# Seven block products for eight in eight dense stages of a four-block model, and two edits in its gated delta rule

## The reference

```python
h_lat = layer_norm(DEEPNORM_ALPHA * h_lat + mod_lat[2] * y_lat, ln1_g[i], ln1_b[i])
f_lat = swiglu(modulate(h_lat, mod_lat[3], mod_lat[4]), w_ffn_in[i], w_ffn_out[i])
# gated delta rule, per token
# S_t = exp(g_t) (I - beta_t k_t k_t^T) S_{t-1} + beta_t k_t v_t^T,  o_t = S_t^T q_t
```

## Time and profile before

| | |
|---|---|
| median of three runs | 5027.18 us |
| profiled execution | 5031.29 us |
| its span, first to last instruction | 5028.8 us |
| TensorE matmul busy | 4424.2 us (88%) |
| VectorE busy | 1856.6 us (37%) |
| ScalarE busy | 1095.0 us (22%) |
| GpSimd busy | 1299.0 us (26%) |
| mean granted TensorE clock | 0.927 |
| moved over HBM | 104 GB/s over the span |

### The profile page before, as it was taken

The page is one execution under the profiler, slowest core; times in us unless marked ns, Lnnn a source line. Parts: engine busy times, 40 slices in busy tenths (PEclk is TensorE's granted clock), DMA queues, the critical chain, the costliest instruction groups (busy, mean ns, idle before and its releaser), DMA issues. The chain is left out here.

```text
span 5028.8 us, 50281 instructions
## 1 busy us (share of the span) xinstructions
PE 4424.2 (88%) x18452; PEld 2709.6 (54%) x18452; DVE 1856.6 (37%) x3562; ACT 1095.0 (22%) x2335; POOL 1299.0 (26%) x1510
## 2 busy tenths in 40 slices
PE   7889899999898656888989999988899888677998
PEld 4566555555455545775434444556655465563443
DVE  6523555511455672432047502034400209900001
ACT  3143200000211542443010001016600122140001
POOL 1100499876000388200039300020000000350000
PEclk9999999999898776888999999999999999778999
DMA  5401466643110244332248512100011153773221
GB/s 185 151 1 54 122 193 201 190 139 120 42 50 31 78 151 119 82 86 66 72 131 247 191 69 73 56 32 1 0 50 45 59 182 127 249 218 111 76 74 67
DMA packets 245067, 526.64 MB, mean 105 GB/s; under 512 B 141088, under 2 KB 147744, under 8 KB 215328
## 3 DMA queue, kind: packets, MB, share of 16 engines
q1 hardware_dynamic: 190944, 341.35, 20.8%
q0 software_dynamic: 53664, 182.75, 12.0%
q10 hardware_dynamic: 288, 0.32, 0.0%
HBM read 429.42 MB, written 94.77 MB: 104 GB/s over the span
## 5 line engine op out<-in xcount | busy, mean ns | idle before, releaser
L195 PE MATMUL P<-hu,ring 128*128 128x512 f32 (+1 forms) x4672 | 1667.9, 520 | 49.4 <-ACT hu L360 22.5
L195 PEld LDWEIGHTS P<-hu,ring 128*128 128x128 f32 x4672 | 891.7, 191 | 825.3 <-issue 762.6
L195 PE MATMUL P<-area,ring 128*128 128x512 f32 (+1 forms) x3104 | 1162.7, 537 | 54.6 <-PEq L1631 28.5
L195 PEld LDWEIGHTS P<-area,ring 128*128 128x128 f32 x3104 | 593.9, 192 | 622.3 <-issue 600.3
L416 POOL TENSOR_TENSOR fold<-mod,vec 128x16 f32<-128x16 f32 (+1 forms) x5 | 1.0, 209 | 1356.0 <-SPq L395 1114.5
L2364 DVE SCALAR_TENSOR_TENSOR hu<-hu,tmp 128x512 f32 (+3 forms) x48 | 45.1, 939 | 749.8 <-ACT tmp L2358 749.8
L1537 POOL TENSOR_TENSOR area<-area 128x512 f32<-128x512 f32 (+2 forms) x128 | 235.6, 1841 | 10.0
L2358 ACT ACTIVATE tmp<-P,mod 128x512 f32<-128x512 f32 x72 | 41.3, 615 | 821.2 <-PE P L195 821.2
L1931 DVE SCALAR_TENSOR_TENSOR area<-area 128x1024 f32<-128x1024 f32 x98 | 214.6, 2190 | 12.1 <-ACT area L2007 7.8
L1536 POOL TENSOR_TENSOR area<-area 128x512 f32<-128x512 f32 (+2 forms) x128 | 210.7, 1646 | 0.0
L1535 POOL TENSOR_TENSOR area<-area 128x512 f32<-128x512 f32 (+2 forms) x128 | 202.2, 1579 | 27.8 <-DMA area<-in_s_bn 23.3
(11 more groups left out here) (331 smaller groups left out, 5268.5 us busy)
## 6 DMA issues: line engine op xcount, KB each, us to landing
ring<-in_w_ffn_in SPq DMA_DIRECT2D x44, 1024.0 KB, 5.9
ring<-s_c POOLq DMA_DIRECT2D x32, 1152.0 KB, 6.3
area<-in_w_mod SPq DMA_DIRECT2D x56, 512.0 KB, 3.7
stat<-in_w_mod SPq DMA_DIRECT2D x48, 512.0 KB, 3.5
ring<-in_w_ffn_out SPq DMA_DIRECT2D x16, 1408.0 KB, 6.0
s_c<-area POOLq DMA_DIRECT2D x32, 576.0 KB, 4.0
area<-s_fa POOLq DMA_DIRECT2D x64, 256.0 KB, 7.6
area<-in_s_bn POOLq DMA_DIRECT2D x64, 256.0 KB, 8.3
```

The lines of the kernel that those rows point to most:

```text
L195: last = nc.tensor.matmul(c.P[:, 2 * s + j, a:b], c.ring[:, slot, (j * kt + k) * 128:(j * kt + k + 1) * 128], x[:, k, a:b], start=k == 0, ...
```

## The change

`dense_seven` takes the place of `dense` in the eight stages named above. It splits the group's weights (two output tiles x two halves of the input tiles) and the input (two halves of the input tiles x two halves of the tokens, n = 384 or 256) into 2 x 2 blocks and forms the four output blocks from seven block products in Winograd's variant of Strassen's algorithm. The four sums of input blocks (t1 to t4) are made once per stage, the four sums of weight blocks (s1, s2, a11 - a21, s4) once per group, all on VectorE. ScalarE copies three products out of PSUM, VectorE makes five additions, two products accumulate in PSUM. Where a stage has a head, its first group stays as it was ("plain"). The modulation products, the tables and the convolution stay in their stages; in att_qk the modulation rows become a ModStream of two groups. In ffn_in0 and gdn_kv the sums lie in `h`, so `h` goes out to HBM and comes back (`spill`). In ffn_in the multiply reads the up half straight from PSUM.

In gdn_heads `GT` gets three and `DB` four buffers, and GT is made two steps ahead. The small joining products get zero-padded operands and contract over all 128 partitions.

```diff
+def dense_seven(c, name, x, n, act, sums, parts, vec=None, act_frees=True, pool=None, mods=None, late=None, head=None,
+                ready=None, start=None, settle=None, three=None, over=False):
...
+    t1, t2, t3, t4 = sums
+    e1, e5, e7 = parts
+    b11, b12, b21, b22 = (x[:, q * i:q * i + q, n * j:n * j + n] for i in range(2) for j in range(2))
+    wide = lambda slot, i: c.ring[:, slot, 128 * q * i:128 * q * (i + 1)].rearrange("p (a b) -> p a b", a=2)
+    s1, s2, s4 = three or (c.ring[:, 0, 2048:2560].rearrange("p (a b) -> p a b", a=2),
+                           c.ring[:, 1, 2048:2560].rearrange("p (a b) -> p a b", a=2), c.ring[:, :, 2560:2816])
+    col = lambda a, k: a[:, k // 2, 128 * (k % 2):128 * (k % 2) + 128]
+    bank = lambda s, j, h: c.P[:, 2 * s + j, 512 * h:512 * h + n]
+    landed = lambda g, s: (g - s) * 8 + 16 * ((at + s) // 2 + 1)
...
+            def more(sp, g):
+                if isinstance(g, int) and g == 1 and settle:
+                    settle(sp)
+                if mods and (mods.groups == groups or isinstance(g, int) and g < mods.groups):
+                    mods.load(sp, g)
+            stream(c, sp, name, more=more if mods or settle else None)
...
+            def product(to, a, b, fresh):
+                for k in range(q):
+                    last = mm(to, col(a, k), b[:, k, :], start=fresh and k == 0, stop=k == q - 1, skip_group_check=True)
+                return last
...
+                product(bank(s, 0, 0), wide(slot, 0), b11, True).then_inc(one_p, 1)
+                pe.wait_ge(s_made, g * 4 + (1 - 4 * plain))
+                if opening_group:
+                    pe.wait_ge(t_made, 1)
+                product(bank(s, 0, 1), s1, t1, True).then_inc(five_p, 1)
+                pe.wait_ge(s_made, g * 4 + (2 - 4 * plain))
+                if opening_group:
+                    pe.wait_ge(t_made, 2)
+                product(bank(s, 1, 1), s2, t2, True).then_inc(six_p, 1)
+                pe.wait_ge(s_made, g * 4 + (3 - 4 * plain))
+                if opening_group:
+                    pe.wait_ge(t3_made, 1)
+                product(bank(s, 1, 0), wide(slot, 2), t3, True).then_inc(seven_p, 1)
+                pe.wait_ge(s_made, g * 4 + (4 - 4 * plain))
+                pe.wait_ge(five_k, g + (1 - plain))
+                product(bank(s, 0, 1), s4, b22, False).then_inc(s_used, 1)
+                pe.wait_ge(one_k, g + (1 - plain))
+                product(bank(s, 0, 0), wide(slot, 1), b21, False)
+                pe.wait_ge(seven_k, g + (1 - plain))
+                if opening_group:
+                    pe.wait_ge(t_made, 3)
+                product(bank(s, 1, 0), wide(slot, 3), t4, False).then_inc(c.mm_done, 1)
...
+            def body(g, s, first):
+                if not (first and s == 0):
+                    finish(g - 1, 1 - s, g < 3)
+                if plain and first and s == 0:
+                    return
+                eng.wait_ge(one_p, g + (1 - plain))
+                copy(e1, bank(s, 0, 0)).then_inc(one_k, 1)
+                eng.wait_ge(five_p, g + (1 - plain))
+                copy(e5, bank(s, 0, 1)).then_inc(five_k, 1)
+                eng.wait_ge(seven_p, g + (1 - plain))
+                copy(e7, bank(s, 1, 0)).then_inc(seven_k, 1)
...
+                    elif ready:
+                        ready(dve)
+                    if over:
+                        dve.wait_ge(head.settled, 1)
+                    tt(t1, b12, b11, ALU.subtract).then_inc(t_made, 1)
+                tt(s1, a21, a22, ALU.add).then_inc(s_made, 1)
+                if fresh:
+                    dve.wait_ge(t_made, 1)
+                    tt(t2, b22, t1, ALU.subtract).then_inc(t_made, 1)
+                dve.wait_ge(s_made, g * 4 + (1 - 4 * plain))
+                tt(s2, s1, a11, ALU.subtract).then_inc(s_made, 1)
+                tt(a21, a11, a21, ALU.subtract).then_inc(s_made, 1)
+                if fresh:
+                    dve.wait_ge(t_made, 2)
+                    tt(t4, b21, t2, ALU.subtract).then_inc(t_made, 1)
+                dve.wait_ge(s_made, g * 4 + (2 - 4 * plain))
+                tt(s4, a12, s2, ALU.subtract).then_inc(s_made, 1)
...
+            def finish(g, s, first):
+                if not (plain and first and s == 0):
+                    dve.wait_ge(c.mm_done, g + (at + 1))
+                    tt(bank(s, 1, 0), bank(s, 1, 0), e1, ALU.add).then_inc(whole, 1)
+                if vec:
+                    dve.wait_ge(act_done, g + 1)
+                    last = None
+                    for j in range(2):
+                        last = vec(g, j, c.P[:, 2 * s + j, :], c.tmp[:, s, j, :]) or last
+                    last.then_inc(vec_done, 1)
+            def body(g, s, first):
+                if not (plain and first and s == 0):
+                    sums_of(g, s, first)
+                if not (first and s == 0):
+                    finish(g - 1, 1 - s, g < 3)
+                if mods and g < mods.groups:
+                    mods.products(dve, g)
+                if plain and first and s == 0:
+                    return
+                dve.wait_ge(six_p, g + (1 - plain))
+                dve.wait_ge(one_k, g + (1 - plain))
+                tt(e1, bank(s, 1, 1), e1, ALU.add).then_inc(mixed, 1)
+                dve.wait_ge(five_k, g + (1 - plain))
+                dve.wait_ge(seven_k, g + (1 - plain))
+                tt(e5, e5, e7, ALU.add).then_inc(mixed, 1)
+                dve.wait_ge(mixed, g * 2 + (2 - 2 * plain))
+                tt(bank(s, 1, 1), e1, e5, ALU.add)
+                dve.wait_ge(s_used, g + (1 - plain))
+                tt(bank(s, 0, 1), bank(s, 0, 1), e1, ALU.add)
...
@@ elsewhere @@
-            V.tensor_scalar(h[:, k, 0:self.width], h[:, k, 0:self.width], self.gain(k), self.shift(k), ALU.mult, ALU.add)
+            last = V.tensor_scalar(self.to[:, k, 0:self.width], h[:, k, 0:self.width], self.gain(k), self.shift(k), ALU.mult, ALU.add)
+        last.then_inc(self.settled, 1)
...
+            sp.dma_start(c.h[:, :, 0:LAT], c.spill[:, :, 0:LAT]).then_inc(h_back, 16)
             stream(c, sp, "gdn_ba", False)
+            sp.wait_ge(h_back, 16)
...
-    GT = [cut(ring, 3328 + 512 * n, 512).rearrange("p (d v n) -> p d v n", d=2, v=2) for n in range(2)]
-    DB = [cut(ring, 4352 + 512 * n, 512).rearrange("p (d v n) -> p d v n", d=2, v=2) for n in range(2)]
-    V5 = cut(ring, 5376, 192).rearrange("p (u n) -> p u n", u=6)
-    XC = qkv[:, 7, LAT:LAT + 192].rearrange("p (u n) -> p u n", u=6)
+    dvn = lambda x: x.rearrange("p (d v n) -> p d v n", d=2, v=2)
+    GT = [dvn(x) for x in (cut(ring, 3328, 512), cut(ring, 3840, 512), cut(tmp, 1536, 512))]
+    DB = [dvn(x) for x in (cut(ring, 4352, 512), cut(ring, 4864, 512), cut(tmp, 2048, 512), cut(tmp, 2560, 512))]
+    XC, V5 = (cut(ring, 3328 + 768 * n, 768).rearrange("p (b u n) -> p b u n", b=4, u=6) for n in range(2))
     AT = [c.view(at + 512 * n, 2, 2, 128) for n in range(2)]
     KT = [c.view(at + 1024 + 768 * n, 6, 128) for n in range(2)]
...
-    X5 = c.view(at + 2560, 6, 64)
-    V6 = c.view(at + 2944, 6, 64)
+    X5, V6 = (cut(tmp, 768 * n, 768).rearrange("p (d u n) -> p d u n", d=2, u=6) for n in range(2))
...
             sp.wait_ge(zeroed, 1)
+            sp.wait_ge(spread, 2)
             fin_load(0)
...
-                    for d, (of, to) in enumerate(((ev, od), (od, ev))):
+                    for d, to in enumerate((od, ev)):
                         for k in range(6):
-                            last = mm(F0[to, 32 * k:32 * k + 32], six(NTF[of, d])[:, k, to], XC[of, k, :], start=True, stop=True)
+                            last = mm(F0[to, 32 * k:32 * k + 32], six(NTF[:, d])[:, k, to], XC[:, 2 * e + d, k, :], start=True, stop=True)
...
-                if n >= 2:
-                    act.wait_ge(dd, n - 1)
...
-                if n >= 2:
-                    act.wait_ge(ntd, n - 1)
+                if n >= 4:
+                    act.wait_ge(ntd, n - 3)
...
-                copy(flat(V5), F0[:, 0:192]).then_inc(f5_k, 1)
+                got = F0[:, 0:192].rearrange("p (u n) -> p u n", u=6)
+                for b in range(4):
+                    last = copy(V5[32 * b:32 * b + 32, b], got[32 * b:32 * b + 32])
+                last.then_inc(f5_k, 1)
...
-                copy(flat(V6), F0[:, 0:384]).then_inc(f6_k, 1)
+                got = F0[:, 0:384].rearrange("p (u n) -> p u n", u=6)
+                copy(V6[64:128, 0], got[64:128])
+                copy(V6[0:64, 1], got[0:64]).then_inc(f6_k, 1)
...
+            act.wait_ge(spread, 2)
...
-                    dve.wait_ge(dd, n - 1)
-                tt(GT[n % 2][:, 1], tri[:, 1:2, :].broadcast_to([128, 2, 128]),
+                if n >= 3:
+                    dve.wait_ge(dd, n - 2)
+                tt(GT[n % 3][:, 1], tri[:, 1:2, :].broadcast_to([128, 2, 128]),
...
-                if n + 1 < 48:
-                    grown(n + 1)
+                if n + 2 < 48:
+                    grown(n + 2)
...
```

(48 more changed lines are left out.)

213 lines of the change are left out of this document (177 added, 36 removed).

## The result

The changed kernel takes 4980.36 us (median of 7 runs, 4973.05 to 4988.20), the one before 5020.47 (7 runs, 5000.65 to 5035.93): ratio 0.9919, 95% interval 0.990 to 0.9937. It is 40 us faster. The forecast was 5039 and slower; the range held the time, the direction was wrong. The profiled execution, span 4983.4 us against 5028.8, shows where it went.

A forecast was written before the change was run, and what follows sets the result against it. TensorE was taken to pace the dense stages, with VectorE becoming the bound of ffn_in0, ffn_in1 and gdn_kv. The terms -7 +33 -3 -10 +60 -23 -18 -9 -8 +5 -8 summed to +12: 5039 us, range 4962 to 5086.

The forecast's parts named there:

- ffn_in1: Second feed-forward input stage: VectorE beside GpSimd's tables takes 21.5 us a group, so +60 us (bounds +27 and +70).
- ffn_in0: First feed-forward input stage: VectorE beside GpSimd's tables takes 22.5 us a group, so +33 us (bounds -20 and +50).
- gdn_kv: Stage with the convolution, GpSimd quiet: VectorE paces at 20.4 us a group against 20.9 before, so -8 us.
- TensorE's side: All dense_seven stages: wide groups gain 2.6 us, narrow ones 1.5, weight loads hidden; 194 us if TensorE paced them all.
- The rival of exposed loads: Narrow groups: weight loads not hidden beside matmuls, 23.1 us a group, 335 us more, 5374 us; chance 0.01.
- The surcharge of 9.5 us a group: ffn_in1 and ffn_in0: ten VectorE instructions with both inputs in SBUF pay 0.95 us each beside GpSimd's tables.
- the first rival: ffn_in0 and ffn_in1: added sums slip into GpSimd's gaps, giving -20 and +27, total -74, 4953 us; chance 0.23.
- 61 was the point: ffn_in0: rival that GpSimd becomes the bound, from 61 us a table; at 66, 5086 us; chance 0.14.
- The spill: h going out to HBM: 0 in ffn_in0 and ffn_out0, +5 us (0 to 10) at the end of gdn_q.
- The scan: Delta rule's second change, zero-padded operands over all rows: -8 us taken between -35 and +25.
- The rival of the full clock: Delta-rule scan: TensorE gets the full clock, 27 us less than the forecast or somewhat more, 5010 us; chance 0.12.
- The first half: Delta rule's first half: added buffers and two steps ahead give -8 us (0 to -20), new memsets +5.

The follow-up runs named there:

- e4: The changed kernel with the scan's small joining products contracting over their 32 or 64 non-zero rows again, spread operands, memsets and copies kept: 5007.42 us, ratio to before 0.9983.
- e5: The changed kernel with two GT and two DB buffers and one step ahead, as before; memsets and spread operands kept: 4978.70 us, ratio to before 0.9917.

## Why the prediction was wrong

The step that failed is the size of one term: VectorE's quiet work in a group (what it takes without GpSimd beside it), in the three stages where VectorE is the bound. It was put 1.6 to 1.7 us too long in each: 12.4 us in ffn_in1, 13.6 in ffn_in0 and 20.4 in gdn_kv, where the trace has 10.7, 11.9 and 18.8. The mechanism held. One by one:

- **TensorE's side** was right: products at 0.323 and 0.216 us (forecast 0.219), weight loads hidden, a narrow group 12.09 us for 12.3, and every other stage that TensorE paces came within 2 us: mla_out, gdn_z, att_qk, att_z, s5_z. The rival of exposed loads fell with it: by the rule of the Trainium skill, TensorE: Matmul & The Clock Gate, Part 3, a narrow group would be 23.1 us, and the trace has 12.09.
- **ffn_in1** was right in kind and nearly in size. Nine groups beside the tables took 20.6 us each (VectorE's multiplies from 2585.57 to 2770.53) for 21.5, and a table took no longer than before (52.7 us on the mean of three, 54.9 before). The surcharge of 9.5 us a group measured 9.9 (products 4.6, sums 4.1, combinations 1.2, by VectorE's lines of that stretch against their quiet values): 1.1 us for a product, 1.0 for a sum and 0.6 for a combination, so between a price per instruction and one in proportion to length. What slipped is the quiet rest: 20.6 less 9.9 is 10.7, and the forecast had 12.4 (of which it dropped 0.4). With the tables gone, VectorE's timeline has the four products in 5.0 us, start to start, for 5.6:

```profile
2805.56 1.22 DVE L2176 SCALAR_TENSOR_TENSOR area<-area 128x1024 f32<-128x1024 f32 x1
...
2810.57 0.42 DVE L547 TENSOR_TENSOR tmp<-P,tmp 128x256 f32<-128x256 f32 x1
```

- Two sums of the forecast for ffn_in1 don't come out. Its own terms (2817 + 10.6 x 12.4 + 7) end at 2955 and not 2959, which is +56. And at 15.7 us a group its own terms give about +14 as the lower bound and not +27, so the first rival should have stood near 4940 and not at 4953.
- **ffn_in0**: 21.3 us a group (598.32 to 1002.45, 19 groups) for 22.5. The surcharge was 9.4 for 9.5, the quiet rest 11.9 for 13.6 (of which 0.6 was dropped). Over 19 groups the 1.2 us are 23 too much; the opening and the tail took 8 more than I had, in this trace. GpSimd was no bound: a table took 51 to 58 us, and 61 was the point.
- **gdn_kv is the step that failed most**: "With sums 2.8, combinations 2.8, ScalarE's two copies 1.8 and gaps 0.5 that is 20.4". VectorE's timeline of one group:

```profile
1499.86 0.17 DVE L2774 TENSOR_SCALAR area<-vec 128x5 f32<-128x5 f32 x1 [1.58 <-ACT tmp L2762]
...
1511.97 0.55 DVE L547 TENSOR_TENSOR area<-P,area 128x384 f32<-128x384 f32 x1
1512.43 0.55 DVE L550 TENSOR_TENSOR area<-area 128x384 f32<-128x384 f32 x1
...
1513.96 0.68 DVE L508 TENSOR_TENSOR ring<-ring 128x512 f32<-128x512 f32 x1
...
1516.49 0.56 DVE L528 TENSOR_TENSOR P<-P,area 128x384 f32<-128x384 f32 x1
1518.62 0.17 DVE L2774 TENSOR_SCALAR area<-vec 128x5 f32<-128x5 f32 x1 [1.58 <-ACT tmp L2762]
```

Start to start it is 18.76 us: convolution 12.1 for 12.5, five combinations 2.6 for 2.8 (four of them 2.0, the last addition 0.6), sums 2.5 for 2.8, the wait for ScalarE 1.6 for 1.8, and nothing for the 0.5 of gaps. The mechanism held (VectorE is the bound; it has no idle time of length but ScalarE's 1.58); the size did not. Sums and combinations were too long because I multiplied the mean duration, 0.56 or 0.69, by the count: an instruction not held by its predecessor starts before that one's record ends, and the pitch from start to start is 0.47 and 0.61. The gaps, which I added on top, are not there for the same reason. The convolution I read to the end of its last record; it was also 0.26 us shorter than before, and why stays open. Twelve groups of 1.6 make 19 us. The kernel before shows such a pair: in its convolution an instruction of 0.56 us starts at 1587.97 and the next at 1588.45, 0.48 later. I took the durations of the earlier trace rows and never set a pitch beside them.
- **The spill** in gdn_q cost 0.9 for 5; the stage's end stood at 12.0 us where it was 11.0.
- **The scan**: between -35 and +25 I took -8, a point that no row gave, and it was -17: e4 splits it into -24 for the clock and +7.5 for copies and layout. The rival of the full clock had the mechanism; the clock came up to 0.89, not to 1. The first half, +5 for the memsets and -8 for the buffers, came out at +4.8 and -7.7 in the trace of e5, whose runs don't show it.

The sum, +12, missed the traces' -45 by 57 us: gdn_q and gdn_kv 22, ffn_in0 15 (13 to 27, by the scatter of that stage), the scan 9, ffn_in1 7, the rest 5. All have one sign. After what I had dropped from VectorE's quiet work, and with the surcharges as measured, its groups were 0.9, 1.2 and 1.6 us too long, over 9, 19 and 12 groups: 50 us, enough to turn the direction. Part of it is the habit of adding up durations (about a third in gdn_kv, and another third the gaps put on top of them); in the feed-forward stages 0.6 of the 1.7 is the four products, and the rest I can't part.

That the range, 4962 to 5086, held the time is no merit of the mechanism. Most of what I gave to "faster" (0.23 of 0.33) stood on sums that slip into GpSimd's gaps; they didn't, for they took 1.3 to 2.4 us beside it.

## What to carry to other kernels

Work taken from the engine that paces a stage is worth its length only up to the next engine's group. Work that out per group, from start-to-start times of a back-to-back stretch and not from durations, and beside whatever else uses the same memory. Where a faster form loads a second engine, put that engine's other work into the stages that don't have the form: here this was worth 100 us, more than twice the change itself. Look then at the third engine in the stage that takes the work: the tables of ffn_out0 got slower and ended the block. A queue that carries both weights and work paced by VectorE has to fit inside a group.
